# GpSimd's row scaling in the attention stages: a scalar operand for each partition in place of a repeated column, and a one-column product behind each wait

## The reference, cut to what matters

```
def _attend(q, k, v, q_pos, k_pos, chunk_causal, c_q=None, c_k=None):
    s = jnp.einsum('bqhd,bkhd->bhqk', q, k) * (q.shape[-1] ** -0.5)
    if c_q is not None:
        s = s + (c_q[:, :, :, None] - c_k[:, :, None, :])
    s = jnp.where(mask[None, None], s, -jnp.inf)
    p = jax.nn.softmax(s, axis=-1).astype(v.dtype)
    return jnp.einsum('bhqk,bkhd->bqhd', p, v)
```

## Time and profile before

| | us |
|---|---|
| median of 3 runs (lowest to highest) | 2337.15 (2335.46 to 2337.54) |
| the profiled execution's own time | 2339.32 |
| its span | 2337.5 |
| PE busy | 2236.7 (96% of the span) |
| DVE busy | 1710.8 (73%) |
| ACT busy | 1075.9 (46%) |
| POOL busy | 315.0 (13%) |

### The profile page before, as it was taken

One profiled execution on the slowest core, in us unless ns is written; L12 is line 12 of the kernel. 1 busy time (PEld: TensorE's weight loads), 2 busy tenths in 40 slices (PEclk: granted clock), 3 DMA queues, 4 the chain that ended last, 5 costly groups with the idle time before them and its releaser, 6 DMA issues. The chain is left out here.

```text
span 2337.5 us, 45432 instructions
## 1 busy us (share of the span) xinstructions
PE 2236.7 (96%) x16542; PEld 2149.9 (92%) x16542; DVE 1710.8 (73%) x2707; ACT 1075.9 (46%) x1801; POOL 315.0 (13%) x278
## 2 busy tenths in 40 slices
PE   6999999899988899999999999999989998999997
PEld 5999999889988899999977999999878888999996
DVE  7975984678875896697455994895467858966973
ACT  6532543456764553354223551453247745533541
POOL 0000002045551000000122000001134421000001
PEclk8999999989989999999999999999979999999998
DMA  3222222100002222232223322223212212222221
GB/s 112 93 107 79 108 102 97 36 25 16 14 19 73 72 105 89 86 107 97 79 74 111 109 98 101 80 97 119 66 44 55 56 61 75 91 104 85 108 93 63
DMA packets 72801, 187.44 MB, mean 80 GB/s; under 512 B 40720, under 2 KB 42288, under 8 KB 61440
## 3 DMA queue, kind: packets, MB, share of 16 engines
q1 hardware_dynamic: 71424, 181.67, 22.4%
q0 software_dynamic: 1280, 4.49, 0.5%
HBM read 178.79 MB, written 7.35 MB: 80 GB/s over the span
## 5 line engine op out<-in xcount | busy, mean ns | idle before, releaser
L628 PE MATMUL ps<-xs_hi,w_hi 128*128 128x272 f32 x1408 | 411.2, 292 | 20.7 <-DVE scratch L1910 9.5
L630 PE MATMUL ps<-xs_hi,w_lo 128*128 128x272 f32 x1408 | 409.1, 291 | 0.0
L629 PE MATMUL ps<-xs_lo,w_hi 128*128 128x272 f32 x1408 | 408.3, 290 | 0.0
L1248 ACT ACTIVATE w_hi<-raw 128x1408 fp32r<-128x1408 f32 (+4 forms) x123 | 146.0, 1188 | 491.9 <-PE ps L662 238.0
L1277 ACT ACTIVATE w_hi<-w_blocks 128x1024 fp32r<-128x1024 f32 x176 | 186.8, 1061 | 323.6 <-PE ps L630 159.5
L628 PE MATMUL ps<-xs_hi,w_hi_more 128*128 128x272 f32 x1056 | 305.8, 290 | 3.1 <-ACT scratch L1325 2.5
L629 PE MATMUL ps<-xs_lo,w_hi_more 128*128 128x272 f32 x1056 | 305.2, 289 | 0.0
L628 PEld LDWEIGHTS ps<-xs_hi,w_hi 128*128 128x128 f32 x1408 | 267.6, 190 | 25.6 <-DVE scratch L1910 7.5
L662 PE MATMUL ps<-hid_hi,w_hi 128*128 128x256 f32 (+1 forms) x1312 | 271.1, 287 | 3.6 <-DVE hid_lo L1821 3.6
L662 PE MATMUL ps<-hid_lo,w_hi 128*128 128x256 f32 (+1 forms) x1312 | 270.6, 287 | 0.0
L662 PE MATMUL ps<-hid_hi,w_lo 128*128 128x256 f32 (+1 forms) x1312 | 270.4, 287 | 0.0
(11 more groups left out here) (266 smaller groups left out, 5073.4 us busy)
## 6 DMA issues: line engine op xcount, KB each, us to landing
w_blocks<-w_ffn_in SPq DMA_DIRECT2D x88, 1024.0 KB, 4.8
raw<-w_ffn_out SPq DMA_DIRECT2D x64, 704.0 KB, 4.1
raw<-w_b_kv SPq DMA_DIRECT2D x16, 512.0 KB, 3.5
raw<-w_a_out SPq DMA_DIRECT2D x8, 512.0 KB, 3.5
raw<-w_b_q SPq DMA_DIRECT2D x8, 512.0 KB, 3.5
raw<-w_b_out SPq DMA_DIRECT2D x8, 512.0 KB, 3.5
raw<-w_a_in SPq DMA_DIRECT2D x4, 672.0 KB, 4.1
raw<-w_a_qup SPq DMA_DIRECT2D x8, 288.0 KB, 2.7
```

The costliest lines, as they stand in the source:

```text
L628: pe.matmul(out, lhs[0], rhs[0], start=start, stop=False, skip_group_check=more)
L629: pe.matmul(out, lhs[0], rhs[1], start=False, stop=False, skip_group_check=more)
L630: return pe.matmul(out, lhs[1], rhs[0], start=False, stop=stop, skip_group_check=more)
L1248: act.activation(wh[par][:, 0:n], raw[par][:, 0:n], ACT.Copy).then_inc(w_hi, 1)
```

## The change

A new tile `rcol` of four columns is allocated. In `normalise`, each `tensor_tensor` that multiplied the tile's rows by a column of `stat` repeated over all the keys becomes a `tensor_scalar` with the same column as its operand for each partition. Ahead of it stands a new `tensor_tensor` of one column: the same reciprocal times a constant column of -0.5, written to `rcol`, which nothing reads. The wait for DVE's reciprocal now stands ahead of this product. The semaphore for the finished tile is counted up by the `tensor_scalar`.

```
+        rcol = sb("rcol", [P, 4])
...
                     for u in range(4):
                         c = ST_RI + 5 * hh + u
                         pool.wait_ge(*st["dve"].at(f"r{hh}{u}", p))
+                        pool.tensor_tensor(rcol[:, u:u + 1], stat[:, c:c + 1], neghalf[:, 0:1], ALU.mult)
                         x = prob[:, P_OFF[u]:P_OFF[u] + P_W[u]]
-                        pool.tensor_tensor(x, x, stat[:, c:c + 1].to_broadcast([P, P_W[u]]), ALU.mult
-                                           ).then_inc(st["pool"].sem, 1)
+                        pool.tensor_scalar(x, x, stat[:, c:c + 1], None, ALU.mult).then_inc(st["pool"].sem, 1)
```

## The result

The changed kernel takes 2387.63 us (median of 4 runs, 2381.28 to 2389.99) against 2337.35 for the kernel before: ratio 1.021, 95% interval 1.0192 to 1.0228, some 50 us slower. The forecast was 2337.5 with a range up to 2345; it was wrong.

What follows compares the result with a forecast made beforehand. PE, busy for 96% of the span, bounds the kernel. POOL's longer chains cost nothing within slack and 0.03 + 0.03 + 0.17 = +0.2 us at three bare places: 2337.15 + 0.2, rounded to 2337.5 us; range 2334.5 to 2345.

Steps and rivals of the forecast that it cites:

- The price of the scalar form: POOL's replaced scalings: 0.20 us fixed plus 1.15 ns for a column; four tiles with products 3.07 us against 2.90.
- the far end: POOL's scalings priced like the form with two streamed inputs, 2.56 ns for a column.
- the prediction's own mark of 1.05 us: Sign in the changed profile: a 512-column POOL row above 1.05 us makes the step on the price wrong.
- rival B: POOL's scalar form runs like two streamed inputs or worse, four tiles 4.88 us: +21 us, 2358; chance 0.11.
- The products: 128 new one-column products on POOL, 0.20 us each: 0.8 us for four tiles, 0.6 for three.
- The slack: POOL's fourth scaling to PE's transpose: stage A head 0 0.3 us, head 1 2.5; stage B 0.8 and 2.1.
- The conversion of waits to time: POOL's growth beyond PE's slack adds its own length to the time: +0.2 us, from the three bare places.
- the prediction's upper end: Scalings at 2.56 ns for a column and products at 0.40 us on POOL: together +35 us.
- DVE and the shared access: DVE's two-SBUF-input line beside POOL's chain may shift by some tenths in 6 pairs, at most 2 us; counted as nothing.
- rival C: POOL pays 0.76 us at each change between kinds of instruction: some 110 us more; chance 0.02.

Runs made afterwards that it cites:

- the filled kernel: The changed kernel with matmuls whose result is overwritten ahead of PE's wait for head 0's scalings (14 in stage A, 7 in stage B): 2368.93 us, ratio 1.0131.
- the kernel with 14 products: The kernel before, old scalings kept, with 2, 3, 4 and 5 one-column products ahead of the four tiles: 2398.87 us, ratio 1.0255.
- the kernel with the powers: The kernel before, old scalings kept, with a power of 2, 3, 3 and 3 columns ahead of the four tiles: 2421.85 us, ratio 1.0351.

## Why the prediction was wrong

*The price of the scalar form: the step that failed first.* The prediction took 1.15 ns for a column, "nearest to the copies" because one input is streamed. It is 2.60, just beyond the far end that the prediction had worked out, 2.56, and the fixed part is 0.27 us in place of 0.20. The 512-column row, 1605 ns, crosses the prediction's own mark of 1.05 us for this step. The number of streamed inputs was the wrong measure of nearness: a constant operand costs the same. The far end had a chance of 0.11 as rival B, under "nothing in the trace speaks for it but the lack of a row". An operation that the trace does not show deserved more than that.

*The products:* right. 0.16 us from start to start, 0.21 in the row. That the chain of four is 4.88 us, to the digit what rival B gave, is partly luck. Rival B summed durations; the same sum of the measured rows is 4.39 + 4 x 0.208 = 5.22 us, but the records on POOL's timeline overlap by some hundredths at each step, and this pair's are a little shorter than the means. For the same reason the old chain was 2.75 us where the prediction counted 2.90, so the growth is 2.13 us and not 2.0.

*The slack:* right for the middle pairs, if a little small: head 0 in stage A took a growth of 2.13 us with a wait of 1.66, so it had nearly 0.5 us and not 0.3. Rival B gave waits of 1.7 us in stage A and 0.9 in stage B; measured 1.57 to 1.75, and 0.72 to 0.81. The last pair of stage B and head 0 of the last pair of stage A were missed; they wait 1.11 and 1.39 us.

*The conversion of waits to time: the step that failed second, and it was in no rival.* For just this chain rival B gave +21 us. PE's waits for POOL did grow by 21.6 us. The time grew by 50, more even than the +35 us of the prediction's upper end, which had dearer products. The sum had no term for the clock, though the kernel before showed its low level where PE had waited longest, behind the 2.87 us of the earlier trace rows:

```profile
690.00:695.00 5.00, 5.00 (x23) 4.89 (x23) 3.00 (x7) 2.15 (x7) 0.00 (x0) 0.50 0.00 0
695.00:700.00 5.00, 5.00 (x20) 4.23 (x19) 2.61 (x9) 2.22 (x7) 2.78 (x4) 0.50 0.00 2
```

The two profiled spans differ by 49.9 us. PE is busy 32.2 us more for the same matmuls and idle 17.7 us more: 21.6 more for POOL's scalings, some 4 less for the rest. By place, 14.7 + 17.9 us are in the middle of the stages. PE's waits for the scalings there are 12.2 us, and the filled kernel gave back 16.0. The other 17.3 us are mostly at the ends of the stages, where PE's waits for the scalings grew by 9.3 us; head 1's waits there had no filler, and how the rest splits was not measured.

*DVE and the shared access:* counted as nothing. The re-timing that the prediction named did happen: the instruction of the earlier trace rows went from 884 to 177 ns in the median, and the one behind it from 176 to 466. So DVE is through with both 2.56 us after the start of POOL's chain, where it was 3.00. No loss can be laid to it in the changed kernel; in the experiments the shared access lengthened POOL's chain.

*Changes between kinds of instruction (rival C):* excluded. The first product took 0.68 us, the median one 0.19.

## What to carry to other kernels

When an instruction's form has no row in the trace, bound its price by the dearest neighbour and ask what that costs; do not choose by likeness. When PE is the busy engine, a wait opened on it costs its length and, in many cases, as much again in clock: here 21.6 us of waits became 50 us. And a helper engine at 13% can hold the time, if its chain ends within half a microsecond of PE's need: read the gap between its end and PE's use, pair by pair, the first and the last pair too.

## What the runs showed of the hardware that was not expected

- GpSimd's TENSOR_SCALAR on float32 costs 2.60 ns for a column plus 0.27 us with an operand for each partition, and 2.60 plus 0.20 with a constant. TENSOR_TENSOR with a repeated column costs 1.67 plus 0.20. The form with one streamed input is the slower one. The Trainium skill ("GPSIMD Engine Reference", Performance versus the Vector engine) gives a tight loop some 1.8 cycles for an element and the two-input one 2.6, by which the one-input form should be faster; the measurement decides.
- DVE's TENSOR_TENSOR with two SBUF inputs and GpSimd's TENSOR_TENSOR hold each other up, in the order in which they come: 0.88 us for 0.18 on DVE, 1.50 for 1.04 on GpSimd. In the changed kernel DVE's L1812 ran inside a GpSimd TENSOR_SCALAR (588.02 to 589.26, 1.24 us) and neither was longer. DVE's one-input L2201 ahead of it was, 0.47 us for 0.18, and 0.88 beside GpSimd's TENSOR_TENSOR in the kernel with 14 products; why is open:

```profile
588.16 0.47 DVE L2201 TENSOR_SCALAR stat<-stat 128x18 f32<-128x18 f32 x1
588.55 0.68 DVE L1812 TENSOR_TENSOR w_lo<-raw,w_hi 128x512 fp32r<-128x512 f32 x1
```

- Short powers on GpSimd: 0.69 us for two columns and 0.85 for three, in the timeline of the kernel with the powers, against 1.95 for ten.
